# Stage one of a three-layer forward pass on Trainium2: q and k of a pair of heads projected as one unit of 768 columns

## The reference, cut to what matters

```
qkv = (h @ w_qkv).reshape(B, S, 3, N_DIL, N_HEADS, HEAD_DIM)     # 3 dilations, 16 heads, 64 wide
q = rope(rmsnorm(qkv[:, :, 0], q_gain)); k = rope(rmsnorm(qkv[:, :, 1], k_gain)); v = qkv[:, :, 2]
for g, (window, dil) in enumerate(((128, 1), (512, 4), (2048, 16))):
    o[g], m[g], d[g] = band_attention(q[:, g], k[:, g], v[:, g], dil, window)
attn = sum over g of (d * exp(m - max)) normalised, times o      # one softmax over three key sets
x = x + attn @ w_o
```

## Time and profile before

| | |
|---|---|
| median of three runs | 1024.41 us |
| span of the profiled execution, first to last instruction | 1023.2 us |
| TensorE matmuls busy | 1018.9 us (100% of the span), 8026 instructions |
| VectorE busy | 880.5 us (86%) |
| ScalarE busy | 687.1 us (67%) |
| GpSimd busy | 349.1 us (34%) |
| weights read | 183.40 MB at 179 GB/s |
| one pair of stage one, from the q transposes of pair 2 to those of pair 3 | 30.4 us |

### The profile page before, as it was taken

The page is one execution under the profiler, slowest core; times in us unless marked ns, Lnnn a source line. Parts: engine busy times, 40 slices in busy tenths (PEclk is TensorE's granted clock), DMA queues, the critical chain, the costliest instruction groups (busy, mean ns, idle before and its releaser), DMA issues.

```text
span 1023.2 us, 22239 instructions
## 1 busy us (share of the span) xinstructions
PE 1018.9 (100%) x8026; PEld 960.4 (94%) x8026; DVE 880.5 (86%) x1535; ACT 687.1 (67%) x1267; POOL 349.1 (34%) x370
## 2 busy tenths in 40 slices
PE   9999999999999999999999999999999999999998
PEld 9999999999999999999999999999998999999998
DVE  7977778787799988887888999988897879999886
ACT  7776766766766665677786766656697776665663
POOL 5312221112255533342111556433350025654332
PEclk9999999999999999999999999999999999999999
DMA  9744465556476666526364566666544536666651
GB/s 318 256 152 151 144 186 155 159 175 205 149 236 195 219 188 202 170 94 217 126 192 153 185 206 213 199 194 193 157 123 135 166 125 213 219 206 195 196 163 42
DMA packets 57753, 183.40 MB, mean 179 GB/s; under 512 B 6352, under 2 KB 9680, under 8 KB 57424
## 3 DMA queue, kind: packets, MB, share of 16 engines
q1 hardware_dynamic: 56816, 181.52, 55.8%
q10 hardware_dynamic: 864, 0.92, 0.3%
HBM read 181.36 MB, written 1.05 MB: 178 GB/s over the span
## 4 chain that ended last, share of the span: by engine, by line
PE 99%; DMA 0%; DVE 0%; ACT 0%; DVEq 0%; issue 0%
PE ps L455 23%; PE ps L457 12%; PE ps L714 10%; PE ps L716 10%; PE ps L715 9%; PE ps L1902 6%; PE ps L1903 6%; PE ps L1904 6%; PE ps L1363 2%; PE ps L1365 2%; PE ps L1364 2%; PE ps L640 1%; PE ps L911 1%; PE ps L806 1%; PE ps L949 1%; PE ps L894 1%
## 5 line engine op out<-in xcount | busy, mean ns | idle before, releaser
L423 DVE TENSOR_TENSOR w_lo<-w_raw,w_hi 128x1024 fp32r<-128x1024 f32 (+2 forms) x369 | 441.2, 1213 | 31.9 <-ACT w_hi L415 31.5
L415 ACT ACTIVATE w_hi<-w_raw 128x1024 fp32r<-128x1024 f32 (+2 forms) x369 | 353.5, 972 | 121.7 <-PE ps L457 102.4
L455 PE MATMUL ps<-xg,w_hi 128*128 128x512 f32 x1056 | 362.8, 390 | 0.0
L457 PE MATMUL ps<-xg,w_lo 128*128 128x256 f32 x1056 | 291.5, 276 | 0.0
L455 PEld LDWEIGHTS ps<-xg,w_hi 128*128 128x128 f32 x1056 | 198.2, 188 | 38.7
L2027 POOL TENSOR_TENSOR prob_t<-prob_t,qkT 128x256 f32<-128x256 f32 x63 | 111.1, 1763 | 257.2 <-ACT prob_t L1948 257.2
L457 PEld LDWEIGHTS ps<-xg,w_lo 128*128 128x128 f32 x1056 | 198.2, 188 | 0.1
L714 PE MATMUL ps<-w_hi,xg 128*128 128x384 f32 (+1 forms) x556 | 192.5, 346 | 0.0
L716 PE MATMUL ps<-w_hi,xg 128*128 128x384 f32 (+1 forms) x556 | 187.3, 337 | 0.0
L715 PE MATMUL ps<-w_lo,xg 128*128 128x384 f32 (+1 forms) x556 | 185.7, 334 | 0.0
L1902 PE MATMUL ps<-g_hi,w_hi 128*128 128x256 f32 x528 | 146.0, 276 | 0.0
(11 more groups left out here) (196 smaller groups left out, 1382.0 us busy)
## 6 DMA issues: line engine op xcount, KB each, us to landing
w_raw<-w_stream SPq DMA_DIRECT2D x228, 512.0 KB, 3.8
w_raw<-w_stream SPq DMA_DIRECT2D x137, 384.0 KB, 3.6
w_raw<-w_stream SPq DMA_DIRECT2D x4, 392.0 KB, 3.1
con<-consts SPq DMA_DIRECT2D x1, 1024.0 KB, 6.8
x_all<-x_t SPq DMA_DIRECT2D x4, 256.0 KB, 5.1
conv_taps<-taps SPq DMA_DIRECT2D x1, 1024.0 KB, 7.2
w_raw<-w_stream SPq DMA_DIRECT2D x4, 192.0 KB, 4.5
x_all<-x_a SPq DMA_DIRECT2D x3, 256.0 KB, 5.6
```

The costliest lines, as they stand in the source:

```text
L415: nc.scalar.activation(w_hi[s][:, 0:w], w_raw[s][:, 0:w], ACT.Copy).then_inc(w_hi_done, 1)
L423: nc.vector.tensor_tensor(w_lo(c)[:, 0:w], w_raw[s][:, 0:w], w_hi[s][:, 0:w].bitcast(F32), ALU.subtract).then_inc(w_lo_done, 1)
L455: nc.tensor.matmul(bank(b, 0, 2 * TOK), w_hi[s][:, k * P:(k + 1) * P], xg[:, k, :, :].rearrange("p h t -> p (h t)"), start=(k == 0), stop= ...
L457: last = nc.tensor.matmul(bank(b), w_lo(c)[:, k * P:(k + 1) * P], xg_hi[:, k, :], start=False, stop=(k == KT - 1), skip_group_check=True)
```

## The change

q and k of a pair become one unit of 768 columns. A chunk of it is one k-tile with 768 columns, in the order k1, k2, q0, q1, q2, k0 (128 columns each), so that a pair has eight such chunks (o = 0 to 7) and four chunks of v (o = 8 to 11) as before. A k-tile and a token tile take per term one product of 512 columns (bank 0 or 1) and one of 256 (half of bank 2), where there were two products of 384. v goes to banks 3 and 4. Transposes, scores and values are laid into banks 4 to 7 and the free ends of banks, with new waits. q and k are now both complete at the end of chunk 7, and their squares, norms and the q transposes move. Above all:

```
-    SA_BANK, PVA_BANK = 4, 7
+    TURN_BANK, QK_BANK, VA_BANK = 6, 2, 3
+QK_PARTS = (slice(0, QK_TAIL), slice(QK_TAIL, QCHUNK))          # 256 and 512 columns
+    SCORE_PLACES = ((5 * 512 + UNIT, 7 * 512), ((VA_BANK + 1) * 512 + UNIT, 6 * 512 + UNIT))
+    def qk_term(n, x, w, part, t, start=False, stop=False):
+        k = n % KT
+        return nc.tensor.matmul(qk_out(part, t), xg[:, k, x, t * P:(t + 1) * P], w[:, QK_PARTS[part]],
+                                start=start and (part == 1 or t == 0), stop=stop, skip_group_check=True)
+    def qk_chunk_pe(eng, p, k):
+        a, n = att[0], 3 * UCH * p + k
+        eng.wait_ge(w_lo_done, n + 1)
+        ...
+        elif k == 0:
+            eng.wait_ge(a.nm, 4 * p)
+        for t in range(2):
+            for part in (1, 0):
+                qk_term(k, 0, w_hi[s], part, t, start=(k == 0))
+            ...
+    def v_chunk_pe(eng, p, q):
+        ...
+        if q == 0 and p > 0:
+            v_wait(eng, 0, p - 1)
+            eng.wait_ge(a.ptr, 2 * p - 1)
     def qt_pe(eng, pr):
+        if pr > 1:
+            eng.wait_ge(a.olo, pr - 1)
     def score_a_pe(eng, pr):
-        if pr > 0 and not joint(pr - 1):
-            eng.wait_ge(a.olo, pr)
-        if pr == 0:
-            v_wait(eng, 0, 0)
+        v_wait(eng, 0, pr)
     def prob_t_a_pe(eng, pr, qt):
+        if qt == 1:
+            eng.wait_ge(a.ptr, 2 * pr + 1)
     def pv_a_pe(eng, pr):
+        past(eng, a.olo, pr, 0, None)
     def square_act / norm_dve:
+            for src, o0, o1 in unit_parts(st, u, t, w):          # k has two parts: 128 and 256 columns
     def prob_t_a_act(eng, pr, qt):                               # query tile 0 has two copies of 256 columns
     def mask_a_dve(eng, pr, qt):
-        eng.wait_ge(a.score, 2 * pr + qt + 1)
+        eng.wait_ge(a.score, 2 * pr + 2)
+        past(eng, a.pv, pr, 0, None)
```

The lists of the engines:

```
     def att_a_pe(eng):
-            if o in (5, 6) and p > 0:
-                prob_t_a_pe(eng, p - 1, o - 5)
-            if o == 7 and p == PAIRS_AB - 1:
-                pv_a_pe(eng, p - 1)
-            if o == (9 if p > 0 else 11):
+            if o in (5, 7) and p > 0:
+                prob_t_a_pe(eng, p - 1, (o - 5) // 2)
+            if o == 10:
                 qt_pe(eng, p)
...
         score_a_pe(eng, p)
+        pv_a_pe(eng, p - 1)
         out_second(eng, 0, 0, UPPER)
         out_second(eng, 0, 1, UPPER)
         out_whole(eng, 0, 2)
-        ...
+        out_whole(eng, 0, 3)
         prob_t_a_pe(eng, p, 0)
         out_first(eng, 0, 4, LOWER)
+        out_first(eng, 0, 5, LOWER)
         prob_t_a_pe(eng, p, 1)
         out_second(eng, 0, 4, UPPER)
         out_first(eng, 0, 6, LOWER)
-        out_first(eng, 0, 7, LOWER)
+        pv_a_pe(eng, p)
         out_second(eng, 0, 5, UPPER)
         out_second(eng, 0, 6, UPPER)
+        out_first(eng, 0, 7, LOWER)
         out_second(eng, 0, 7, UPPER)
     def att_a_act(eng):
-            if o == (4 if p > 0 else 7):
-                square_act(eng, 0, 3 * p, UNIT)
-            if o == (5 if p > 0 else 8):
-                norm_act(eng, 0, 2 * p, 0, 2 * NDIL)
-            if o in (6, 7) and p > 0:
-                prob_t_a_act(eng, p - 1, o - 6)
+            if o in (6, 8) and p > 0:
+                prob_t_a_act(eng, p - 1, (o - 6) // 2)
+            if o == 8:
+                square_act(eng, 0, 3 * p, UNIT)
+            if o == 9:
+                square_act(eng, 0, 3 * p + 1, UNIT)
+                norm_act(eng, 0, 2 * p, 0, 2 * NDIL)
+            if o == 10:
+                norm_act(eng, 0, 2 * p + 1, 1, 2 * NDIL)
+            if o == 11:
                 q_act(eng, 0, p)
     def att_a_dve(eng):
+            if o == 2 and p > 0:
+                mask_a_dve(eng, p - 1, 0)
+                mask_a_dve(eng, p - 1, 1)
+            if o == 8:
+                sums_dve(eng, 0, 2 * p, 0, 2 * NDIL)
+            if o == 9:
+                sums_dve(eng, 0, 2 * p + 1, 1, 2 * NDIL)
+                norm_dve(eng, 0, 2 * p, 3 * p, 0, 0, 2 * NDIL)
+            if o == 10:
+                norm_dve(eng, 0, 2 * p + 1, 3 * p + 1, 1, 1, 2 * NDIL)
```

More of the change, by code:

```diff
@@ L56 @@
 UCH = KT // 2
+QK_TAIL = 2 * P
+QK_PARTS = (slice(0, QK_TAIL), slice(QK_TAIL, QCHUNK))
 A_QKV = 0
@@ L644, in term @@
             return last
[L646 to L669 removed]
+        eng.wait_ge(w_hi_done, c + 1)
@@ new lines, in early_chunk_pe, with qk_out @@
+        eng.wait_ge(x_hi, k0 + 2 * n + 2)
+        for kk in range(2):
+            term(0, w_hi[s], kk)
+        eng.wait_ge(x_lo, k0 + 2 * n + 2)
+        for kk in range(2):
+            term(1, w_hi[s], kk)
+        eng.wait_ge(w_lo_done, c + 1)
+        for kk in range(2):
+            last = term(0, w_lo(c), kk, ends=(2 * n + kk == KT - 1))
+        last.then_inc(tiles, 1)
+    def qk_out(part, t):
+        return bank(QK_BANK, t * QK_TAIL, QK_TAIL) if part == 0 else bank(t, 0, 512)
+    def qk_term(n, x, w, part, t, start=False, stop=False):
+        k = n % KT
+        return nc.tensor.matmul(qk_out(part, t), xg[:, k, x, t * P:(t + 1) * P], w[:, QK_PARTS[part]],
+                                start=start and (part == 1 or t == 0), stop=stop, skip_group_check=True)
@@ new lines, in qk_early_pe, with term @@
+    def qk_early_pe(eng, n):
+        s = n % RING
+        def term(x, w, part, start=False):
+            for t in range(2):
+                last = qk_term(n, x, w, part, t, start=start)
+            return last
+        if n < HALVES:
+            for part in range(2):
+                eng.wait_ge(half_hi if part == 0 else w_hi_done, n + 1)
+                eng.wait_ge(x_hi, n + 1)
+                term(0, w_hi[s], part, start=(n == 0))
+                if part == 0:
+                    eng.wait_ge(half_lo, n + 1)
+                    term(0, w_lo(n), part)
+                    eng.wait_ge(x_lo, n + 1)
+                    term(1, w_hi[s], part)
+                else:
+                    term(1, w_hi[s], part)
+                    eng.wait_ge(w_lo_done, n + 1)
+                    last = term(0, w_lo(n), part)
+        else:
+            eng.wait_ge(w_hi_done, n + 1)
+            eng.wait_ge(x_hi, n + 1)
+            for part in range(2):
+                term(0, w_hi[s], part)
+            eng.wait_ge(x_lo, n + 1)
+            for part in range(2):
+                term(1, w_hi[s], part)
+            eng.wait_ge(w_lo_done, n + 1)
+            for part in range(2):
+                last = term(0, w_lo(n), part)
+        last.then_inc(tiles, 1)
@@ new lines, in qk_chunk_pe @@
+    def qk_chunk_pe(eng, p, k):
+        a, n = att[0], 3 * UCH * p + k
+        s = n % RING
+        eng.wait_ge(w_lo_done, n + 1)
+        if p == 0:
+            eng.wait_ge(x_lo, k + 1)
+        elif k == 0:
+            eng.wait_ge(a.nm, 4 * p)
+        for t in range(2):
+            for part in (1, 0):
+                qk_term(k, 0, w_hi[s], part, t, start=(k == 0))
+            for part in (1, 0):
+                qk_term(k, 0, w_lo(n), part, t)
+            for part in (1, 0):
+                last = qk_term(k, 1, w_hi[s], part, t, stop=(k == KT - 1))
+            if k == KT - 1 and t == 0:
+                last.then_inc(a.unit, 1)
+        last.then_inc(tiles, 1)
@@ L924, in pv_a_pe @@
                 both = prob_t[:, h, 0:2, P + t * CLASS:P + (t + 1) * CLASS].rearrange("p q (c l) -> p c q l", c=2)
-                nc.tensor.matmul(out[lo:hi, :], band[:, 0, lo:hi], both, start=(not joint(pr) and t == 0), stop=False,
+                nc.tensor.matmul(out[lo:hi, :], band[:, 0, lo:hi], both, start=(t == 0), stop=False,
                                  skip_group_check=True)
@@ L1407, in att_a_pe @@
             p, o = divmod(n, 3 * UCH)
-            unit_chunk_pe(eng, 0, n)
+            if n < UCH:
+                qk_early_pe(eng, n)
+            elif o < KT:
+                qk_chunk_pe(eng, p, o)
+            else:
+                v_chunk_pe(eng, p, o - KT)
             if n == 7:
```

220 lines of the change are left out of this document (104 added, 116 removed).

## The result

Five runs of the changed kernel took 1056.20 to 1059.37 us, median 1058.72, against 1024.29: ratio 1.0328 (95% interval 1.0316 to 1.0339), so slower, by 34.4 us. The forecast was 1047 with a range of 1037 to 1057: the direction and the main cause, a wait for rotated q in each pair, were right; the size was not, and the time lies just outside the range.

The account below looks back on a forecast made before the run. TensorE, busy 99% of the span at full clock, was taken as the bound. Terms -2.6 + 24 + 1.1 + 0.8 - 0.4 = +22.9 us brought the 1023.2 us span to 1046.1, with 1.2 around it 1047 us; range 1037 to 1057.

Parts of the forecast that it names:

- Term 2: At the q transposes TensorE waits 3.0 us for rotated q in each of eight pairs: +24 us (18 to 32).
- the clock falls: Rival: products after each q-transpose wait run at half speed for 3.2 us, 1.6 us more per wait: 1060 us; chance 8%.
- another format is used: Argument against the clock rival: the slow warm-up products at TensorE's start, 0.225 us each, use another format than later ones.
- Term 1: q and k products: couples of 512 and 256 columns are 6.7 ns cheaper than two of 384: -2.6 us (nothing to -2.6).
- The linear rule of the Trainium skill: Warm distance of isolated TensorE products is columns / 2.4 + 2.5 ns; both couples would cost 325 ns.
- What the stall covers: Waits for k's norm and rotation, scores, masks and DMA cost nothing while TensorE waits at the q transposes.
- Term 3: Behind the last pair, the scores wait for the whole of v: +1.1 us (0.5 to 1.5).
- Term 5: At the start, a smaller first part and one k-tile of x needed, not two: -0.4 us (-1.1 to +0.3).
- Term 4: Into the feed-forward stage, VectorE's adds and low parts of x come later: +0.8 us (0 to 1.5).
- no wait: Rival: rotated q is ready in time at the q transposes and the change pays: 1022 us; chance 6%.
- a shorter wait: Rival: TensorE waits only some 1 us per pair at the q transposes: 1031 us; chance 6%.
- Around the span: Time outside the profiled span, taken as 1.2 us and added to the forecast span of 1046.1 us.

Follow-up runs that it names:

- experiment 4: The changed kernel with the q transposes one chunk earlier in TensorE's list, behind chunk 9 and not 10: 1083.67 us, ratio 1.0580.
- experiment 5: The kernel of experiment 1 with the q transposes behind chunk 9 and not 10: 1047.50 us, ratio 1.0221.
- experiment 1: The changed kernel with ScalarE squaring and norming q before copying the probabilities, k's squares later, VectorE's list reordered to match: 1031.43 us, ratio 1.0071.
- experiment 8: The kernel of experiment 1 with 512-column products ahead of 256-column ones and work reordered to remove the three remaining waits: 1026.29 us, ratio 1.0016.
- experiment 15: The kernel before, with only the offset of the weights' low part in its ring buffer varied by feed-forward chunk, same work and values: 1038.70 us, ratio 1.0140.
- experiment 10: The kernel before, with the 256-column product of feed-forward gate couples written to the neighbouring bank: 1024.64 us, ratio 1.0002.

## Why the prediction was wrong, point by point

- **Term 2**, the wait for rotated q, 24 us forecast: right in place, number and cause, 21.4 measured, within its bounds of 18 to 32. Per pair 2.65 and not 3.0: squares of q took 0.74 and not 0.91, squares of k 0.84 and not 1.24, and from the first logarithm to GpSimd it was 2.28 and not 2.23; the rotation took 3.33, as the earlier trace rows said (3.26).
- **The step that failed: the clock as a rival, not a term.** The case "the clock falls" had 8% and, for all eight waits, 13 us. The clock did fall, behind three to five waits of eight, for 1.7 us each (forecast 1.6): 5 to 8.5 us. Without them the runs would lie at 1050 to 1052 (an estimate, half of 3.41 us for each stretch), within the range and 3 to 5 us from the forecast. The step argued from a full granted clock in the only slow stretch seen that the clock wouldn't answer to idleness. That reading didn't hold. The trace's records of the granted clock begin only 6.8 us behind the first instruction, and the page prints full where it has none. The products of the earlier trace rows run on at half pace up to there, in the very format of the kernel:

```profile
5.51 0.84 PE L640 MATMUL ps<-w_lo,xg 128*128 128x384 f32 x2
6.15 1.16 PE L640 MATMUL ps<-w_hi,xg 128*128 128x384 f32 x4
```

(6.15 - 5.51) / 2 = 0.32 us, what the slow stretches behind the waits show at 0.50, against 0.17 from 6.98 us on. So "another format is used" was no argument either, and the slow start lasted 5.7 us from the first warm-up product; the forecast's 3.2 is the warm-up from its first start to its last, and that it came out near the 3.41 measured is luck. And before the change TensorE never stood still once it ran, so the trace could not say what a wait does; an unseen thing that acts on each of eight waits belonged into the range as a bound, and its whole price beside the 24, not into a case of its own. The Trainium skill's rule cited there, that idle gaps bring the lower clock back, is borne out by all eight gaps of experiment 4 (4.3 us and more) and by five of the ten between 2.2 and 3.4 us in the changed kernel and experiment 5; the six of 1.64 didn't do it.
- **Term 1**, the second step that failed, forecast -2.6: about +1.5 (384 couples x 0.004). The price was read from another stage. Its lower bound ("nothing, if the gain is not there") excluded a loss without a reason. The linear rule of the Trainium skill that the forecast cites would have made it 0, nearer, though both couples are longer than its 325 ns.
- **What the stall covers**, forecast 0: right. With the stall gone (experiment 1) none of it waits either, at a pair's period of 30.6.
- **Term 3**, +1.1: 1.2 in the list of waits. **Term 5**, -0.4: about -0.2.
- **Term 4**, +0.8: 2.0, above its bound of 1.5. The third and fourth k-tile start 0.95 and 0.88 behind the one before, where 0.34 is the couple; VectorE makes their low parts at the 0.86 of the earlier trace rows each. That is some 1.3 us, and none of it comes back: the split of the next chunk's weights (L425) is queued behind those low parts on VectorE and holds up the second chunk, some 0.3 us more; the last 0.3 are the three chunks at 0.350 in place of 0.340.
- **The rivals** of no wait and of a shorter wait: refuted by the eight waits. The 1022 of the first was added up wrongly: it takes 0.5 for terms 3 and 4, which the sum has at 1.9, so by its own terms it was 1023.3. In experiment 8, where the waits are gone, the time is 1026.3: the gain of term 1 isn't there.
- **Around the span** 1.2 us were taken; the profiled execution has 1.8.

## What to carry to other kernels

When a chain of work is moved between two points of an in-order engine, write out every list it passes through: three steps ahead of q's norm (a copy, a split and the squares of k), none of them needed by q, cost 27 us with the slow stretches behind the waits, and the order alone gave them back. A new idle time on TensorE above some 2 us must be priced twice, as itself and as the stretch at half clock that may follow it. A distance between products read from one stage is not a price of their shape in another: here it moved by 4% with the place of an operand in memory and with what ran just before, so compare forms with the operands where they will lie and in the stream in which they will run.

## What the runs showed of the hardware

- The granted clock falls in the records of stage one only during a wait or right behind one: never after 1.64 us (0 of 6), sometimes after 2.2 to 3.4 (3 of 8 in the changed kernel, by their mean clocks up to 5 of 8 in other runs, and 2 of 2 in experiment 5), always after 4.3 to 5.5 (8 of 8, experiment 4). A slow stretch was 3.41 us or, in half of those eight, 6.83. The longest wait of the profile after (pair 7, 3.4 us) had none behind it, so length isn't all; what else decides is open.
- At the start 384 columns took 0.32 us up to 6.8 us with a printed clock of 1.00, the same 0.32 as at 0.50 behind the waits. The trace has no record of the clock before that moment, so the page's row doesn't tell of slowness at the start.
- The place of the low part of the weights, or of x, changes a couple of 768 columns from 0.340 to up to 0.353 us. In experiment 15 that was some 8 us, and 6 more came in products whose own operands lay where they had been: 0.119 us for 256 columns and not 0.114, depending on the chunk ahead of them. The bank written to changes nothing in the feed-forward stage (experiment 10).
- GpSimd's operations on 96 columns took 0.38 us while VectorE scaled k out of PSUM (96.12 to 97.4), those on 192 columns 1.17 and 1.40 while VectorE split weights between memory buffers (95.25 and 97.43); alone, 192 columns take 0.60. The rotation of k right behind, with VectorE idle, took 1.96 us from 98.89 where that of q took 3.33. In the kernel before one of the 96-column operations took 1.10 beside such a split. So it matters which operation of VectorE runs beside GpSimd. That was read from rows, not tested.
